# Weighing the values of two attention heads at once on the two column halves of TensorE, with the rows divided on POOL

## What is computed

```python
MLA_HEADS = 8
MLA_QK = MLA_NOPE + MLA_ROPE      # 64 + 32
MLA_V = 64

def causal_block_attention(q, k, v):      # q,k (B,H,S,96), v (B,H,S,64)
    def one_block(args):
        qi, s0 = args
        sc = jnp.einsum('bhqd,bhkd->bhqk', qi.astype(jnp.float32), kf) * scale
        sc = jnp.where(key_idx[None, :] <= q_idx[:, None], sc, -jnp.inf)
        p = jax.nn.softmax(sc, axis=-1)
        return jnp.einsum('bhqk,bhkd->bhqd', p, vf)

h = h + jnp.concatenate([o_gla, o_mla], axis=-1) @ w_out[l]
```

## Time and profile before

| what | value |
|---|---|
| time, median of 3 runs | 3275.32 us (3274.34 to 3284.05) |
| the profiled execution, its own time | 3268.24 us |
| its span in the profile | 3266.5 us, 38694 instructions |
| busy: PE, PE's weight loads | 3069.2 us (94%), 2428.7 us (74%) |
| busy: DVE, ACT, POOL | 1878.1 us (57%), 951.3 us (29%), 805.5 us (25%) |
| the attention's 64 periods | from 338 us to 580 us of the span; the products with `w_out` in full flow from 596.3 us |

### The profile page before, as it was taken

One profiled execution on the slowest core, in us unless ns is written; L12 is line 12 of the kernel. 1 busy time (PEld: TensorE's weight loads), 2 busy tenths in 40 slices (PEclk: granted clock), 3 DMA queues, 4 the chain that ended last, 5 costly groups with the idle time before them and its releaser, 6 DMA issues. The chain is left out here.

```text
span 3266.5 us, 38694 instructions
## 1 busy us (share of the span) xinstructions
PE 3069.2 (94%) x15406; PEld 2428.7 (74%) x15406; DVE 1878.1 (57%) x2775; ACT 951.3 (29%) x1837; POOL 805.5 (25%) x478
## 2 busy tenths in 40 slices
PE   7999888888999999999899999998998999999888
PEld 6777777767788888888677777776676777777666
DVE  4334566534653253354578888888444267777773
ACT  3232444324210000001333333334222244444431
POOL 3221000241333233323232323232232211121111
PEclk9998999989999999999999999999999999999899
DMA  3102000010111111112211212122331110001021
GB/s 124 34 32 95 13 1 14 33 58 27 63 45 52 45 45 52 52 45 77 71 46 39 78 40 77 40 78 96 111 97 69 42 33 27 27 26 33 7 78 65
DMA packets 47738, 170.26 MB, mean 52 GB/s; under 512 B 5200, under 2 KB 5472, under 8 KB 46688
## 3 DMA queue, kind: packets, MB, share of 16 engines
q1 hardware_dynamic: 45856, 161.85, 14.7%
q0 software_dynamic: 1728, 6.29, 0.5%
HBM read 145.06 MB, written 23.07 MB: 51 GB/s over the span
## 5 line engine op out<-in xcount | busy, mean ns | idle before, releaser
L193 PE MATMUL acc<-x_hi,w_hi 128*128 128x512 f32 x2048 | 841.7, 411 | 48.9 <-POOL w_lo L188 22.4
L186 POOL CAST w_hi<-w_raw 128x1024 fp32r<-128x1024 f32 x217 | 236.3, 1089 | 2388.7 <-PE acc L195 1431.0
L194 PE MATMUL acc<-x_lo,w_hi 128*128 128x512 f32 x2048 | 818.4, 400 | 0.0
L195 PE MATMUL acc<-x_hi,w_lo 128*128 128x512 f32 x2048 | 817.6, 399 | 0.0
L188 POOL TENSOR_TENSOR w_lo<-w_raw,w_hi 128x1024 fp32r<-128x1024 f32 x217 | 544.9, 2511 | 17.4
L193 PEld LDWEIGHTS acc<-x_hi,w_hi 128*128 128x128 f32 x2048 | 390.5, 191 | 156.6 <-issue 39.9
L195 PEld LDWEIGHTS acc<-x_hi,w_lo 128*128 128x128 f32 x2048 | 390.2, 191 | 95.0
L194 PEld LDWEIGHTS acc<-x_lo,w_hi 128*128 128x128 f32 x2048 | 391.0, 191 | 89.6 <-issue 2.4
L2513 DVE SCALAR_TENSOR_TENSOR acc<-ev_upad,cols,acc 128x1024 f32<-128x1024 f32 x232 | 298.3, 1286 | 5.0
L193 PE MATMUL aux<-x_hi,w_hi 128*128 128x512 f32 x464 | 198.9, 429 | 2.1 <-POOL w_lo L188 2.1
L195 PE MATMUL aux<-x_hi,w_lo 128*128 128x512 f32 x464 | 184.3, 397 | 0.0
(11 more groups left out here) (506 smaller groups left out, 4965.3 us busy)
## 6 DMA issues: line engine op xcount, KB each, us to landing
w_raw<-in_stream SPq DMA_DIRECT2D x217, 512.0 KB, 3.4
h<-in_x SPq DMA_DIRECT2D x16, 512.0 KB, 9.5
spill_h<-h SPq DMA_DIRECT2D x8, 512.0 KB, 5.2
spill<-ev_zst SPq DMA_DIRECT2D x8, 512.0 KB, 3.0
h_even<-spill_h SPq DMA_DIRECT2D x8, 512.0 KB, 8.3
ev_zr<-spill SPq DMA_DIRECT2D x8, 512.0 KB, 3.5
spill_h<-h_even SPq DMA_DIRECT2D x8, 512.0 KB, 5.2
h<-spill_h SPq DMA_DIRECT2D x8, 512.0 KB, 4.5
```

The costliest lines, as they stand in the source:

```text
L186: pool.tensor_copy(k.w_hi[slot][:], k.w_raw[slot][:]).then_inc(k.w_split, 1)
L193: pe.matmul(out, w_hi, x_hi, start=start, stop=False)
L194: pe.matmul(out, w_hi, x_lo, start=False, stop=False)
L195: return pe.matmul(out, w_lo, x_hi, start=False, stop=stop)
```

## The change

Heads are weighed in pairs, one on each column half of PE, and with the roles of the operands swapped. In an even head the turned exponents are only kept, in `mla_kept` (36 blocks). In an odd head each group is weighed together with the same group of the even head: the values (128x64) are now the weights of the array and the turned exponents (128x128) stream through, the even head's into partitions 0 to 63 of one PSUM bank, the odd head's into 64 to 127. The result has the features of two heads on the partitions and tokens on the columns, as `m_hi` and `m_lo` want it, so `turn_o`, `output` and `mla_o` are gone. ACT copies each 128x128 result to `m_hi` (`high`) and DVE subtracts to `m_lo` (`low`), in later periods; the result has one bank for most t and another for t = 4 and 6.

Since the sums now lie along the wrong axis, the exponents are divided before they are turned: DVE takes the reciprocal of one block's sums (`invert`), and POOL multiplies `mla_p` by it in place. Every turn comes one period later. The projections move from periods 0 and 1 to periods 2 and 3. `exponent` stands behind the first `copy_qk` in ACT's order.

```diff
-    o_tok = k.at("mla_o", 80, [P, TT, H * MLA_V])
+    kept = k.at("mla_kept", 80, [P, TT * (TT + 1) // 2, P])
+    def turned_out(t):
+        bank = 2 if t in (4, 6) else 3
+        return aux[:, bank * HALF:bank * HALF + P]
+    def read_at(n):
+        return TT * (n // TT // 2) + n % TT
...
         @block.gpsimd
         def _(pool):
-            stream_splits(k, pool, wa + 1, cb + 1)
+            stream_splits(k, pool, wa + 1, wa + 6)
+            for n in range(TT * H):
+                t = n % TT
+                pool.wait_ge(s["inverse"], n + 1)
+                pool.tensor_scalar(pr[:, t % 2, 0:(t + 1) * P], pr[:, t % 2, 0:(t + 1) * P], st[:, 27, t % 2:t % 2 + 1], None,
+                                   ALU.mult).then_inc(s["divided"], 1)
+            stream_splits(k, pool, wa + 6, cb + 1)
...
             def turn(h, i):
-                pe.wait_ge(s["exped"], TT * h + t + 1)
+                pe.wait_ge(s["divided"], TT * h + t + 1)
...
             def weigh(h, i):
                 t, g = GROUPS[i]
+                n = TT * (h // 2) + t
+                wait_used(pe, ("p", h - 1, i))
                 wait_used(pe, ("p", h, i))
                 if i == 0:
                     pe.wait_ge(s["vt_done"], h + 1)
-                    pe.wait_ge(s["o_read"], h + 1)
+                if t == 4 and g[0] == 0:
+                    pe.wait_ge(s["z_copied"], 4 * min(h + 3, H))
+                if g[0] == 0 and n:
+                    pe.wait_ge(s["m_lo"], n if t < 4 else n - 1)
+                out = turned_out(t)
                 for j, kb in enumerate(g):
-                    mm = pe.matmul(aux[:, 3 * HALF + t * MLA_V:3 * HALF + (t + 1) * MLA_V], pT[:, i % 2, j * P:(j + 1) * P],
-                                   vt[h % 2][:, kb, :], start=kb == 0, stop=kb == t)
+                    pe.matmul(out[0:MLA_V, :], values_of(h - 1)[:, kb, :], kept[:, kept_at(t, kb), :], start=kb == 0, stop=kb == t)
+                    mm = pe.matmul(out[MLA_V:P, :], values_of(h)[:, kb, :], pT[:, i % 2, j * P:(j + 1) * P], start=kb == 0, stop=kb == t)
                 mm.then_inc(s["pv_done"], 1)
...
-            def turn_o(j):
...
-            def period(h, t):
...
+            def period(n):
+                (h, t), (hm, tm) = divmod(n, TT), divmod(n - 1, TT)
+                more, ahead, i = h + 1 < H, h + 2 < H and t in (2, 3), FIRST_GROUP[tm]
+                if n + 1 < TT * H:
+                    scores(*divmod(n + 1, TT))
+                if ahead:
+                    project(h + 2, 2 * t - 4)
+                if n:
+                    turn(hm, i)
+                    if hm % 2 and i:
+                        weigh(hm, i - 1)
+                    if hm and hm % 2 == 0 and i == 0:
+                        weigh(hm - 1, NG - 1)
+                if ahead:
+                    project(h + 2, 2 * t - 3)
                 if more and t in (5, 6):
                     turn_qk("qk"[t - 5], h + 1, 0)
+                if n and tm >= 4:
+                    turn(hm, i + 1)
+                    if hm % 2:
+                        weigh(hm, i)
                 if more and t in (5, 6):
                     turn_qk("qk"[t - 5], h + 1, 1)
...
-            def output(h):
...
+            def invert(h, t):
+                n = TT * h + t
+                dve.wait_ge(s["exped"], n + 1)
+                if n >= 2:
+                    dve.wait_ge(s["divided"], n - 1)
+                dve.reciprocal(st[:, 27, t % 2:t % 2 + 1], sums_of(h)[:, t:t + 1]).then_inc(s["inverse"], 1)
+            def low(n):
+                p, t = divmod(n, TT)
+                dve.wait_ge(s["m_hi"], n + 1)
+                cols = slice(t * P, (t + 1) * P)
+                dve.tensor_tensor(m_lo[:, p, cols], turned_out(t), m_hi[:, p, cols].bitcast(F32), ALU.subtract).then_inc(s["m_lo"], 1)
...
             def period(n):
+                if n + 1 < TT * H:
+                    tile_max(*divmod(n + 1, TT))
+                if n < TT * H:
+                    invert(h, t)
+                if n and tm >= 4:
+                    copy_turned(dve, hm, FIRST_GROUP[tm])
+                if n >= 3 and (n - 3) // TT % 2:
+                    low(read_at(n - 3))
+                if h + 1 < H and t < 6:
+                    PREPARE[t](h + 1)
```

More of the change, by code:

```diff
@@ L1183, in block_mla @@
     names = ("loaded h_back squares gained sums k_turned g_hi g_lo wo_half added z_copied_pe z_copied chain chain_act stats_in stats_out "
[L1184 removed]
+             "qk_ready vt_done scores row_max maxed exped inverse divided ring_full ring_act ring_dve pv_done squared_roots m_hi m_lo").split()
     s = {n: k.own(f"m_{n}") for n in names}
@@ L1197, in ring_order @@
                 yield (which, 0, c), ACTE
[L1198 to L1205, removed]
+        for n in range(TT * H + 1):
+            (h, t), (hm, tm) = divmod(n, TT), divmod(n - 1, TT)
+            if n:
+                yield ("p", hm, FIRST_GROUP[tm]), DVEE if tm >= 4 else ACTE
+            for c in range(2):
+                if t in (5, 6) and h + 1 < H:
+                    yield ("qk"[t - 5], h + 1, c), ACTE
+                if n and tm >= 4 and c == 0:
+                    yield ("p", hm, FIRST_GROUP[tm] + 1), ACTE
     USE, freed, counts = {}, [], {ACTE: 0, DVEE: 0}
@@ L1337, in project @@
                     pe.wait_ge(s["z_copied"], h * 4 + tp)
+                if h >= 4 and h % 2 == 0 and tp == 0:
+                    pe.wait_ge(s["m_lo"], TT * (h // 2 - 1) - 1)
                 for u in range(2):
@@ L1525, in period @@
                         mem_norm.square(act, 7)
-            for h in range(H):
-                for t in range(TT):
-                    period(h, t)
-            high(2)
-            high(3)
+            for n in range(TT * H + 1):
+                period(n)
+            high(TT * H // 2 - 1)
             mem_norm.root_of(act)
@@ L1681, in period @@
                     (q_squares, k_squares)[t - 6](h + 2)
-                if not nxt:
-                    low(0)
-                    low(1)
-                if not more and t >= 2:
+                if h == H - 1 and t >= 2:
                     mem_norm.sum(dve, t - 1)
-                if not nxt:
+                if n == TT * H - 1:
                     mem_norm.sum(dve, t)
-            for h in range(H):
-                for t in range(TT):
-                    period(h, t)
-            output(H - 1)
-            low(2)
-            low(3)
+            for n in range(TT * H + 1):
+                period(n)
+            low(TT * H // 2 - 2)
+            low(TT * H // 2 - 1)
             for i in range(KD):
```

133 lines of the change are left out of this document (49 added, 84 removed).

## The result

| | before | after |
|---|---|---|
| time, median | 3272.72 us (6 runs) | 3299.36 us (6 runs, 3296.57 to 3304.06) |
| profiled execution, span | 3268.24, 3266.5 us | 3298.91, 3297.1 us |
| first maximum to last maximum | 241.8 us | 264.9 us |
| last maximum to the first full product with `w_out` | 19.8 us | 16.6 us |

The change made the kernel slower: ratio 1.0077, 95% interval 1.0063 to 1.0092. The forecast was 3274, the range ended at 3292.

What follows compares the result with a forecast made beforehand. The attention stage was taken to be near PE's own work, its big intervals a loop of PE and DVE. PE's 24 us less work against 23 more waiting summed to -1.5 on 3275.3, about 3274 us; range 3263 to 3292.

Steps and rivals of the forecast that it cites:

- the cast's rate: POOL's division priced like its cast of 128x1024, 1041 ns: 0.13 us a block, 1.2 for block row 7, 46 in all.
- Slow POOL: Rival: POOL divides at its two-input operation's rate, 2.4 us for row 7; +15 us, 3290 at the median; chance 0.2.
- a falling clock: Rival: PE stands still more in the attention stage, its clock falls more often; four stretches give +6, 3280; chance 0.1.
- The halves run together: In weighing, two products on PE's column halves take one product's time, 0.22 a pair; rival, halves apart: +27 us, chance 0.05.
- Entering and leaving them: Switching PE between column halves and whole array was estimated at 0.18 us for each of 48 calls of `weigh`.
- The wait for `low`: In periods 4 to 6 of odd heads PE waits 1 to 2 us each; interval t = 6 grows from 5.5 to 7.4.
- An even head's t = 6: Interval from the maximum of block 6 to the next, in even heads: shorter by 0.8, near 4.7 us.
- From the last maximum to the first full product with `w_out`: The attention's end, 19.8 us before, would take about 15.6, -4.2, with only the last row's division, turns and pairs left.
- Head 0: The first head has no earlier head's work to do and its projections move off the start: -3.9 us.
- head 7: The last head has no projections, so its waits for `low` lie open: +1.2 us.
- The odd heads: Three odd heads were each to take 2.0 us more than the 32.15 reckoned for the head before.
- The collisions: DVE and POOL reading SBUF hold each other out for whole instructions, every period: 9 us; rival, hardly any: -10, chance 0.15.

Runs made afterwards that it cites:

- e1: The change with POOL's division cut to one column, so rows are not divided, all else kept: 3272.1 us, ratio 1.0002 to the kernel before.
- e9: The change with POOL dividing only 48 of every 128 columns, the division length the prediction took: 3271.8 us, ratio 0.9998 to the kernel before.
- e4: The change with eight short filler products on PE ahead of the first turn of blocks 4 to 7: 3282.5 us, ratio 1.0034 to the kernel before.
- e3: The change with POOL's division cut to one column and `low` ahead of the maximum on DVE: 3252.9 us, ratio 0.9948 to the kernel before.
- e8: The kernel before with POOL doing the same 64 multiplications on an unused tile, awaited only after the attention: 3284.0 us, ratio 1.0032; run again, 1.0044.

## Why the prediction was wrong

**The step that failed**, as it stood: "I take the cast's rate, since one stream is read, and 0.1 for starting: 0.13 us a block, 1.2 for block row 7, 46 us of POOL in all". It measured 0.28 us and 0.32 a block, 2.84 for row 7. The row it was "nearest" to was chosen by the number of streams; the row of the two-input operation, 2.4 us, was the better one, and even that was not the upper end. The prediction bounded the cost by those two rows and its range by the price at the dearer one, 15 us, which is why 3299 lies outside. The 2.6 cycles an element of the Trainium skill (GPSIMD Engine Reference, Elementwise — side-by-side cycle accounting), set aside there with the 2.2 us worked out from it, were nearer than the cast's row, and still too low; the page gives them for an operation on two tensors.

**The second miss is how that price was worked out.** Slow POOL and a falling clock stood as two rivals, +15 and +6. They are one case: with the long division the clock of the stage is 0.91, and with a short one in the same order 0.97 (e1, e9). e4 puts the clock's part at 10 us or more of the 24 that the attention lost. How the long division brings it about is shown in part only: most spells begin behind waits for ACT or for `low`, which e1 and e9 have too, and e3, with the fewest waits for POOL, has 0.96. The forecast's clock was "0.98 or more". With the division as forecast and the clock nearly so (e9), the forecast was 2 us off.

**Point by point.** The halves run together at 0.22 a pair: right. Entering and leaving them was taken at 0.18 a call:

```profile
603.12 0.33 PE L1344 MATMUL aux<-mats,mla_p 128*128 128x128 f32 x1
603.38 0.32 PE L1361 MATMUL aux<-mla_kept,mla_v 128*64 128x128 f32 x1
603.38 0.32 PE L1362 MATMUL aux<-mla_pT,mla_v 128*64 128x128 f32 x1
...
604.20 0.27 PE L1362 MATMUL aux<-mla_pT,mla_v 128*64 128x128 f32 x1
604.40 1.77 PE L919 MATMUL acc<-mla_kT,mla_qT 96*128 96x512 f32 x4
```

From the transpose to the first pass 0.26, where a transpose takes 0.11, and from the last pass to the scores 0.20 for 0.11: 0.24 a call, 3 us more in all than was taken. The wait for `low`, 1 to 2 us in an odd head, is there (1.93), and t = 6 is 7.53 at full clock for a forecast 7.4. An even head's t = 6 is 4.64 with a short division for a forecast 4.7; in the change its turn of row 4 waits 1.80 for POOL and it is 5.97. From the last maximum to the first full product with `w_out` the change gave 3.2 us of 4.2. Head 0 in e9 is 26.3 for 29.9, -3.7 for a forecast -3.9; head 7 lost 3.2 where 1.2 stood. The odd heads lost 0.9 to 1.3 each in e9 where 2.0 stood.

**The collisions were right in one direction and wrong in the other.** "Each waits until the other's instruction is over" had a price of 9 us. Where DVE comes first it fits: in e1 a division of 0.28 us ended only behind DVE's 0.68, and in the change those of 640 columns took 2.31 for 1.88. Where POOL comes first it doesn't. Beside POOL's 2.20 us division, DVE's operation on two SBUF inputs took 0.79 instead of 0.68 (467.54, above), where waiting for POOL's end at 469.09 would have added 1.5 us; t = 0 is 3.04 in two heads of e9 and 3.33 to 3.37 in four, for a forecast 3.8. The rule of the Trainium skill that stood with it there (SBUF — State Buffer, Who interferes with whom) describes the first case and not the second. With this, the odd heads, and spells at half clock in other places (the kernel before has one in head 2, 1.4 us), e9's attention, from the first maximum to the first full product with `w_out`, is 4.1 us shorter than before's, where -1.5 was summed. So that e9 met the forecast within 2 us is luck in part: terms were off both ways, and the stretches outside the attention took 10 us more in e9's profile than in before's, for which no run shows a reason.

What is open: why executions differ by 10 us and more in layers that nobody changed, and whether POOL has a part in it.

## What to carry to other kernels

Before giving work to an idle engine, price it by a row of that same operation on that engine, and if there is none, let the dearest row near it carry the sum. An idle engine is no free one where another waits for its result: here POOL was four times as slow as DVE, and giving DVE the work, with `low` ahead of the maximum, turned a loss of 0.8% into a gain of 0.2% (0.3% with the short rows left to POOL). And a wait on PE can have two prices, its own length and half clock behind it, so a rival with longer waits and a rival with a lower clock shouldn't be priced apart.

## What the runs showed of the hardware

POOL's multiplication of a 32-bit tile by a number for each row takes 0.28 us and 2.5 ns a column (0.28 for 1 column, 2.84 for 1024), more than its subtraction of two tiles, 2.4 us for 1024; the same instruction on DVE takes 0.74. An operation of DVE on two SBUF inputs that is running holds it up to its end (0.84 us for one column in e1). The other way round, operations of DVE beside it lost 0.1 to 0.5 us and went on, one with a single input among them (L485 in e8, 0.64 for 0.17). Where the earlier rows show waits of microseconds, POOL's instruction was the cast or the subtraction.

A spell at half clock behind a wait of PE reaches into what comes after. Each of the eight in the change's attention followed a wait of PE of 1.8 or 1.9 us, and where PE waited again inside one, 1.3 us for POOL, it lasted about ten microseconds instead of three or four. Not every such wait has a spell behind it: e9 has waits for `low` and ACT of the same length and two spells.
